# Thirteen phases in fp32r products: zero products at the start, tiles in steps of 256, fewer split products, and retention outputs in pairs

## The reference

```python
h = h + 0.5 * swiglu(rmsnorm(h, g), w_gate, w_up, w_down)        # FF = 2816

def hybrid_mixer(u, ...):
    q, k, v, a, b, g_sb, g_conv = split(u @ w_in)                 # 36 panels of 128 columns
    y_sb = stick_breaking_attention(q, k, v) @ w_attn_out
    y_conv = conformer_conv(a, b, ...) @ w_conv_out
    m = sigmoid(g_sb) * y_sb + sigmoid(g_conv) * y_conv
    return m @ w_out

def _retention(xn, w_in, subln, w_out):
    q, k, v, g = split(xn @ w_in)                                 # 4 heads, chunks of 128
    o = _rms(retain(q, k, v), subln)                              # 2048 wide
    return (silu(g) * o) @ w_out
```

## Time and profile before

| | us |
|---|---|
| median of 3 executions | 2171.73 (2171.69 to 2171.99) |
| the profiled execution | 2172.23 |
| its span | 2170.4 |
| TensorE busy | 2159.0 (18139 products) |
| VectorE busy | 1473.0 |
| ScalarE busy | 1202.2 |
| GpSimd busy | 283.9 |

### The profile page before, as it was taken

One profiled execution on the slowest core, in us unless ns is written; L12 is line 12 of the kernel. 1 busy time (PEld: TensorE's weight loads), 2 busy tenths in 40 slices (PEclk: granted clock), 3 DMA queues, 4 the chain that ended last, 5 costly groups with the idle time before them and its releaser, 6 DMA issues.

```text
span 2170.4 us, 48317 instructions
## 1 busy us (share of the span) xinstructions
PE 2159.0 (99%) x18139; PEld 2141.7 (99%) x18139; DVE 1473.0 (68%) x2242; ACT 1202.2 (55%) x1752; POOL 283.9 (13%) x328
## 2 busy tenths in 40 slices
PE   8999999999999999999999999999999999999999
PEld 8999999999999999999999999999999999999999
DVE  6655998665566579876657657976656745686663
ACT  6444786544444368755555546865445535565552
POOL 0001661100100136220020011010010010101000
PEclk9999999999999999999999999999999999999999
DMA  6555435556455554455656655356656655445664
GB/s 233 176 192 167 163 118 175 175 174 198 153 181 186 182 165 142 149 177 193 205 180 194 200 188 170 117 184 191 207 173 195 209 178 180 161 158 195 193 217 131
DMA packets 100401, 386.57 MB, mean 178 GB/s; under 512 B 11312, under 2 KB 12464, under 8 KB 100304
## 3 DMA queue, kind: packets, MB, share of 16 engines
q1 hardware_dynamic: 99648, 383.89, 53.7%
q0 software_dynamic: 368, 1.26, 0.2%
q10 hardware_dynamic: 288, 0.12, 0.0%
HBM read 384.18 MB, written 1.05 MB: 177 GB/s over the span
## 4 chain that ended last, share of the span: by engine, by line
PE 91%; DVE 6%; ACT 2%; issue 1%; DMA 0%; SPq 0%; ACTq 0%; DVEq 0%
PE bank L423 28%; PE bank L416 28%; PE bank L424 28%; DVE wlo L439 2%; DVE bank L1702 1%; PE bank L1056 1%; PE bank L1058 1%; PE bank L1057 1%; ACT whi L432 1%; PE bank L1103 0%; PE bank L770 0%; DVE proj L1688 0%; PE bank L947 0%; PE bank L950 0%; PE bank L949 0%
## 5 line engine op out<-in xcount | busy, mean ns | idle before, releaser
L416 PE MATMUL bank<-u,whi 128*128 128x256 f32 (+2 forms) x3776 | 1062.6, 281 | 7.3 <-DVE u L477 7.3
L423 PE MATMUL bank<-u,whi 128*128 128x256 f32 (+1 forms) x3776 | 1062.1, 281 | 0.0
L424 PE MATMUL bank<-u,wlo 128*128 128x256 f32 (+1 forms) x3776 | 1060.0, 281 | 0.0
L439 DVE TENSOR_TENSOR wlo<-raw,whi 128x1024 fp32r<-128x1024 f32 (+1 forms) x677 | 892.7, 1321 | 186.1 <-ACT whi L432 185.5
L432 ACT ACTIVATE whi<-raw 128x1024 fp32r<-128x1024 f32 (+1 forms) x677 | 743.5, 1112 | 192.3 <-PE bank L424 172.0
L416 PEld LDWEIGHTS bank<-u,whi 128*128 128x128 f32 x3776 | 711.3, 188 | 8.5 <-DVE wlo L439 7.2
L423 PEld LDWEIGHTS bank<-u,whi 128*128 128x128 f32 x3776 | 711.3, 188 | 0.9 <-issue 0.2
L424 PEld LDWEIGHTS bank<-u,wlo 128*128 128x128 f32 x3776 | 711.1, 188 | 0.0
L416 PE MATMUL bank<-hid,whi 128*128 128x256 f32 (+1 forms) x1408 | 394.2, 280 | 0.0
L423 PE MATMUL bank<-hid,whi 128*128 128x256 f32 (+1 forms) x1408 | 394.2, 280 | 0.0
L424 PE MATMUL bank<-hid,wlo 128*128 128x256 f32 (+1 forms) x1408 | 394.2, 280 | 0.0
(11 more groups left out here) (297 smaller groups left out, 2190.8 us busy)
## 6 DMA issues: line engine op xcount, KB each, us to landing
raw<-w SPq DMA_DIRECT2D x552, 512.0 KB, 3.3
raw<-w SPq DMA_DIRECT2D x128, 704.0 KB, 4.8
h<-xT SPq DMA_DIRECT2D x4, 272.0 KB, 5.6
outT<-h SPq DMA_DIRECT2D x8, 128.0 KB, 5.0
consts<-cst POOLq DMA_DIRECT2D x1, 576.0 KB, 5.0
dist<-cst POOLq DMA_DIRECT2D x1, 192.0 KB, 2.8
rdist<-cst POOLq DMA_DIRECT2D x1, 192.0 KB, 3.7
sgain<-small POOLq DMA_DIRECT2D x1, 145.5 KB, 5.4
```

The costliest lines, as they stand in the source:

```text
L416: pe.matmul(out[:, cut:cols], w, x[:, cut:cols], start=first, stop=False, skip_group_check=True)
L423: pe.matmul(out, w_h, x_lo, start=False, stop=False, skip_group_check=True)
L424: return pe.matmul(out, w_l, x_hi, start=False, stop=last, skip_group_check=True)
L439: dve.tensor_tensor(weights(1, n), raw[:, n % RING, 0:COLS[n]].rearrange("p (k c) -> p k c", c=128), weights(0, n), ALU.subtract).then_inc ...
```

## The change

It has five parts. (1) A memset of `sq` and five f32 products of zeros run on TensorE before anything is loaded; the order of the first loads is x, half of panel 0, x, the other half, x, x, then panels 1 to 3 in halves, and ScalarE, VectorE and TensorE work on the first four panels by halves. The first sum of squares goes from GpSimd to VectorE, and GpSimd's loads of constants wait for the fourth high part. (2) In the second mixer the inputs of the last products lie 256 columns apart (`mixed_at`, `attended_at`), and its weights 128. (3) `CUTS` is (0, 128, 0, 0): one product in two parts for each feed-forward, behind the norm. (4) `BEHIND_TERMS` has 7 entries, cut at 128; the mixer's input panels have one cut instead of two, and its end three new ones; attention's output tile 4 has one. (5) Retention's output tiles are made in pairs: the first eight terms for both, then the other eight for both, with a new order on ScalarE and VectorE.

```diff
-CUTS = (0, 252, 128, 0)
-BEHIND_TERMS = [(0, 1), (0, 2), *((t, c) for t in range(1, RT_HEADS + 1) for c in (0, 1)), (RT_HEADS, 5), (RT_HEADS + 1, 1), (RT_HEADS + 1, 2)]
+CUTS = (0, 128, 0, 0)
+BEHIND_TERMS = [(0, 1), *((t, 1) for t in range(1, RT_HEADS + 1)), (RT_HEADS, 5), (RT_HEADS + 1, 1)]
...
+        def mixed_at(l, part, k):
+            if l == 0:
+                return qk[:, KD * part + k, :]
+            at = KD * T * part + SEQ * k
+            return qk[:, :, :].rearrange("p a t -> p (a t)")[:, at:at + SEQ]
...
-            step = GAP_STEP if in_mixer_end(n) else 128
+            step = GAP_STEP if in_first_mixer_end(n) else 128
...
+            for i in range(X_PARTS):
+                sp.dma_start(h[:, X_TILES * i:X_TILES * (i + 1), :], ...).then_inc(x_loaded[i], 16)
+                if i < 2:
+                    load_half(0, i)
+            for n in range(1, RING):
+                for i in range(2):
+                    load_half(n, i)
...
+            pe.wait_ge(zeros_set, 1)
+            for i in range(WARM_UP):
+                pe.matmul(NORM[:, 0:SEQ], sq[:, 0:128], sq[:, 0:SEQ], start=True, stop=True)
...
             for f in range(KD):
                 act_update(act, 0, f)
-            act_split(act, 1)
-            act_split(act, 2)
+                if f in (1, 3):
+                    act_half(act, 0, f // 2)
+            for n in range(1, RING - 1):
+                for i in range(2):
+                    act_half(act, n, i)
...
-                out_proj(y, P + 48, 2)
+                for f in range(KD):
+                    n = P + 48 + 2 * f + RING
+                    act_split(act, n)
+                    act_split(act, n + 1)
+                    act_update(act, y + 1, f)
...
-                out_proj(y, P + 48, 2, 1.0, SEQ)
+                for f in range(KD):
+                    n = P + 48 + 2 * f + RING
+                    dve_split(dve, n)
+                    if f % 2 == 0:
+                        dve_split(dve, n + 1)
+                    if f > 0:
+                        dve_update(dve, y + 1, f - 1)
+                    dve.wait_ge(panel_used, P + 48 + 4 * (f // 2) + 3 + f % 2)
+                    dve.tensor_tensor(h[:, f, W], bank[4 + f % 2][:, 0:SEQ], h[:, f, W], ALU.add).then_inc(h_done, 1)
+                    if f % 2 == 1:
+                        dve_split(dve, n + 1)
+                dve_update(dve, y + 1, KD - 1)
```

More of the change, by code:

```diff
@@ L17 @@
 K8 = KD * 128
+HALF8 = K8 // 2
 K11 = HALF * 128
@@ L598, in _, with group @@
                   .then_inc(x_loaded[i], 16)
+                if i < 2:
[3 more added lines that the diff above has]
+                    load_half(n, i)
             def panels(n0, count, src, d0, cols):
[L603 to L604 removed]
+                def group(it):
+                    for j in range(RING):
                         n = n0 + j
[L606 to L607 removed]
+                        sp.wait_ge(lo_ready, n - RING + 1 + RING * it)
                         sp.dma_start(raw[:, n % RING, 0:cols], src[d0 + j + RING * it, :, :])\
                           .then_inc(raw_loaded[n % RING], 16)
[L610 to L613, removed]
+                with sp.Fori(1 if n0 == 0 else 0, count // RING) as it:
                     group(it)
@@ L643, in gate_up @@
                         n, g = b["P"] + j, b["A"] + j
-                        pe.wait_ge(lo_ready, n + 1 + RING * it)
+                        halves = norm and slow
+                        if halves:
+                            pe.wait_ge(half_lo, j + 1)
+                        else:
+                            pe.wait_ge(lo_ready, n + 1 + RING * it)
                         if g + RING * it >= RING if isinstance(it, int) else True:
@@ L647, in gate_up @@
                         for k in range(KD):
+                            if halves and k == KD // 2:
+                                pe.wait_ge(lo_ready, n + 1)
                             if norm and j == 0 and slow:
@@ L1113, in rt @@
                                       stop=True).then_inc(r_osum, 1)
-                out_proj(y, b["P"] + 48, 2, KD, lambda part, k: ry[:, part, k, :], r_y_ready,
-                         16, SEQ, lag=6)
+                with pe.Fori(0, KD // 2) as it:
+                    for q in range(2):
+                        for j in range(2):
+                            n = b["P"] + 48 + 2 * q + j
+                            if q == 0:
+                                pe.wait_ge(h_done, KD * (y + 1) + j - 1 + 2 * it)
+                            pe.wait_ge(lo_ready, n + 1 + RING * it)
+                            for k in range(KD):
+                                K = q * KD + k
+                                if j == 0 and (K == 0 or K >= KD):
+                                    pe.wait_ge(r_y_ready, KD if K == 0 else K + 1)
+                                mm = products(pe, bank[4 + j][:, 0:SEQ], n, k, ry[:, 0, K, :], ry[:, 1, K, :],
+                                              K == 0, K == 2 * KD - 1)
+                            mm.then_inc(panel_used, 1)
+            pe.wait_ge(zeros_set, 1)
+            for i in range(WARM_UP):
+                pe.matmul(NORM[:, 0:SEQ], sq[:, 0:128], sq[:, 0:SEQ], start=True, stop=True)
             layer = 0
```

89 lines of the change are left out of this document (57 added, 32 removed).

## The result

The changed kernel took 2182.17 us in the median of 18 executions (2169.49 to 2187.64); the kernel before, beside it, 2171.99 us (2170.94 to 2173.37, 18 executions). The ratio is 1.004, 95% interval 1.0031 to 1.0049: slower, where 2167.8 us was forecast. The spread says more than the median. The 18 times of before lie within 2.4 us. Those of the changed kernel lie in groups: 2169.49 once, five from 2175.96 to 2178.63, seven from 2181.97 to 2182.38, four from 2183.86 to 2184.69, and 2187.64. From the first group to the second and from there to the third it is 6 to 7 us; the four near 2184 and the one at 2187.64 fit such steps less well. The profiled execution took 2176.67 us (span 2174.9), so it is one of the second group; no execution of the groups above it was profiled.

The account below looks back on a forecast made before the run. TensorE bounds the kernel: instruction count times rhythm (113.3 or 118 ns) plus a few stalls. Terms -0.9 - 0.9 - 1.2 - 1.7 + 0.75 = -3.95 us, from the median 2171.73, gave 2167.8 us; range 2165.6 to 2170.4.

Parts of the forecast that it names:

- The step that failed: Feed-forwards: a 128 part right behind the norm brings back the 113.3 ns rhythm behind three norms, -0.3 us.
- rival (d): Feed-forwards: the 128 part behind a norm leaves the slow rhythm on, 7.0 us each, three giving 2188.8; chance 0.05.
- Second mixer's end: Steps of 256 bring the products behind the stall to 113.3 ns; less new parts and stalls, -1.2 us.
- Rival (a): Second mixer's end: the rhythm doesn't follow the tiles' steps, so the mixer gives 0: 2169.0; chance 0.13.
- Start: Kernel's start: zero products bring full clock near 6.5, the new load order the first norm at 16.95: -1.7 us.
- Retention's input: Retention's input panels: six parts fewer and faster rhythm, less some panels turning slow, -0.9 us (bounds -1.2 and -0.4).
- Outputs in twos: Retention's outputs: old stall gone, -0.35, but a new stall before the next norm, +1.1: net +0.75 us.
- Feed-forwards, the part I kept: Five feed-forwards of 256 columns: one part fewer in each, 0.113 us a part, -0.6 us together.
- Attention: Attention's outputs: a new part at f = 4, but VectorE sets the stage's end: 0, at most +0.11 us.

Follow-up runs that it names:

- e2: The changed kernel with a second 128+128 part, in panel 2 of each 256-column feed-forward, beside the one behind the norm: 2170.15 us.
- e4: The changed kernel with no product of a feed-forward in two parts: 2189.82 us.
- e5: e1 without the five zero products at the start: 2175.95 us.
- e8: e1 with the second mixer's end in its old tile steps, the changed kernel's parts kept: 2176.33 us.
- e16: e9 without the zero products at the start: 2169.62 us.
- e14: e9 with the second mixer's end in its old tile steps, parts kept: 2169.97 us.
- e11: e9 with the start of the kernel before (no zero products, whole loads and splits): 2170.20 us.
- e1: The changed kernel with each feed-forward's 128+128 part moved from panel 1, behind the norm, to panel 2, a running stream: 2169.65 us.
- e9: e7 with VectorE's eight products of h by the norm's factor in the second feed-forward spread over eight tiles instead of four: 2168.74 us.
- e6: e1 with six zero products at the start instead of five: 2170.35 us.
- e13: e9 with each feed-forward's 128+128 part back in panel 1, straight behind the norm's product: 2173.53 us.
- e7: e1 with VectorE's last u at the retention's end ahead of the low part instead of behind it: 2169.52 us.

## Why the prediction was wrong

**The step that failed** is in the feed-forwards: "With the 128 part right behind the norm, 22 products x 4.5 ns x 3 = -0.3 us", and the weight of rival (d), 0.05. The mechanism and price of (d) stood there: 1560 products x 4.5 ns = 7.0 us; the profile has 1557 slow products and +6.8. What I set against it, "every 128 part in the trace is followed by 113.3 within four products", was evidence from parts in a running stream alone, which the same paragraph says. Over all 18 profiles (kernels before and changed, and the experiments), leaving out mixers with the old steps, 158 parts of 128+128 stood behind at least six regular products. In panels of feed-forwards, mixer and retention 142 of 142 were followed by 113.3, and 83 of these streams had been slow. In attention's output tile 4 the part never lifted anything: 11 streams came fast and stayed so, 5 came slow (e2, e4, e5, e8, e16) and stayed slow. e2 there, TensorE:

```profile
1416.43 0.28 PE L922 MATMUL bank<-dy_hi,wlo 128*128 128x256 f32 x1
1416.56 0.22 PE L433 MATMUL bank<-dy_hi,dw_hi 128*128 128x128 f32 x1
1416.62 0.27 PE L435 MATMUL bank<-dy_hi,dw_hi 128*128 128x128 f32 x1
...
1417.72 0.28 PE L435 MATMUL bank<-dy_hi,dw_hi 128*128 128x256 f32 x1
1418.07 0.28 PE L435 MATMUL bank<-dy_hi,dw_hi 128*128 128x256 f32 x1
```

The last two starts lie 0.35 us apart over three products, 0.117 each. For comparison with the parts in a stream, here is the first product straight behind an f32 product of `ssq` (seven norms and two such sums a panel later in each profile), by its form:

| first product behind the norm | then fast | then slow |
|---|---|---|
| 128+128 | 33 | 2 |
| 252+4 | 5 | 6 |
| whole | 35 | 81 |

The places differ too, so the five feed-forwards by themselves: 128+128 was followed by fast products in 18 of 20 cases, whole in 32 of 65. At the first and the fourth, whole was slow in 24 of 26 and 128+128 fast in 8 of 8; at the other three the two did alike (30 of 39 and 10 of 12 fast). So the form of that product shifts the odds, and in a feed-forward only the running stream made it certain (no part there failed). The kernel before drew badly at three of its norms and ran only some 22 products slow each time, because a part in the running stream came one panel later; the change saved that part's 0.113 us and put 7.0 at stake five times. (The 23 in 2.40 us of the earlier trace rows, counted as the others, would give 114 ns; it is the starts there, 0.118 us apart, that show the slow rhythm.) At 7 in 50 that is 4.9 us per execution for 0.56 saved.

**What no rival had:** the wait inside the second feed-forward. The forecast priced a part fewer and a fast panel as TensorE's gain and never asked who comes second there. The chain of VectorE and ScalarE does. In the kernel before, TensorE came there 0.2 us later and just didn't wait; and what the wait costs is not its 0.1 us but, in three of seven profiles, the rhythm of all that follows.

**Second mixer's end,** -1.2 forecast, -1.10 by the traces, 1.23 by e14. The stall at 910.49 is there. Behind it the way to the norm takes 40.34 us against 41.29, 0.95 less and not 1.75. Most of the other 0.8 went to three things: the two parts and waits for VectorE, which were in the sum, and a slow stretch, which was not. TensorE waited 0.15 us at 924.83 and 0.08 at 927.94, and 35 products behind the second wait ran at 117.8 until the next part:

```profile
924.83 0.28 PE L442 MATMUL bank<-ao_hi,wlo 128*128 128x256 f32 x1
925.10 0.39 PE L434 MATMUL bank<-ao_hi,whi 128*128 128x256 f32 x1
...
927.94 0.36 PE L434 MATMUL bank<-qk,whi 128*128 128x256 f32 x1
928.13 0.28 PE L441 MATMUL bank<-qk,whi 128*128 128x256 f32 x1
```

Rival (a) falls: the steps count (e8, e14; 0.93 and 1.11 us by the traces).

**Start,** -1.7 forecast, -1.31 in this profile, 1.46 by e11. I put the clock near 6.5. In the changed kernel's profile the 272-column products lie 0.227 us apart until 10.7 and 0.12 after (1.2 and 2.4 GHz):

```profile
6.60:10.40 3.80, 3.80 (x17) 1.00 1.02 347
10.80:17.00 6.20, 6.20 (x52) 1.00 0.90 322
```

That is the exception: of the 13 profiles with zero products 11 have the 0.12 us spacing by 7.3, and only this one and e1's (10.3) have it late. But that the clock is there doesn't bring the norm forward by itself. In e9, with the same start, the full clock was there at 6.65, the first norm at 16.96 (forecast 16.95), and TensorE waited for data instead:

```profile
8.83 0.36 PE L435 MATMUL bank<-u,whi 128*128 128x272 f32 x1 [0.66 <-DVE u L511]
```

Against e9, the late clock cost 0.2 to 0.4 us (norm at 17.17 in e1, 17.38 in the changed kernel), late data 0.7 to 0.9 (e6 and e13: clock by 6.5, norm at 17.62 and 17.90). The forecast had reckoned with one arrival of the data; what it missed in most executions is how late they can be. Over the profiles with zero products the first norm lies between 16.96 and 17.90, and this scatter may be what blurs comparisons of under half a microsecond. The Trainium skill ("TensorE: Matmul & The Clock Gate", Part 1: The HAM clock gate) says that how many products run at the low clock differs between executions of one kernel; the traces agree (full clock at 6.65 in e9 and at 10.7 in the changed kernel, whose starts are the same code).

**Retention's input,** -0.9 forecast, -0.32 by both pairs of traces. The six parts (0.68) and the 70 products behind (4, 5) (0.31) were gained. I allowed +0.2 for panels that turn slow; three panels (t, 0) turned for 29 products each (0.39), panels (0, 2) and (0, 3) for 47 instead of 22 (0.11), (5, 0) for 23 (0.10): +0.60. These terms add up to -0.39. The stated bounds were -1.2 and -0.4, so the -0.32 lies just outside them.

**Outputs in twos,** +0.75 forecast, +0.90 measured: -0.35 to the hundredth, and the new stall with its place (three products before the norm), its releaser (VectorE's u) and its cause (e7). The changed kernel, VectorE and then GpSimd:

```profile
1984.75 0.42 DVE L2168 TENSOR_TENSOR h<-bank,h 128x256 f32<-128x256 f32 x1
1985.13 1.23 DVE L457 TENSOR_TENSOR wlo<-raw,whi 128x1024 fp32r<-128x1024 f32 x1
1986.27 0.83 DVE L510 SCALAR_TENSOR_TENSOR u<-h,gain,u 128x256 fp32r<-128x256 f32 x1
```

```profile
1985.24 1.58 POOL L545 TENSOR_TENSOR sq<-h 128x256 f32<-128x256 f32 x1 [2.04 <-DVE h L2168]
1986.90 0.79 POOL L548 TENSOR_TENSOR ssq<-ssq,sq 128x256 f32<-128x256 f32 x1
```

The order is the forecast one; what was lengthened is not the low part (1.23) but u (0.83, elsewhere 0.48), and GpSimd's square took 1.58, where the one at 1981.76, alone, took 0.62. It starts 0.11 behind the low part and ends 0.46 after it, about as if it had waited for the low part's end and only then run, though 0.46 is less than the 0.62 alone. The Trainium skill ("SBUF — State Buffer", Who interferes with whom) says that VectorE with two SBUF inputs contends with a GpSimd instruction that reads SBUF, and that the ports they share are an exclusive lock. I had set that below the row of 1.63; this pair of rows agrees with it roughly. The sum of squares, whose lateness I had not carried on to the norm, then held the norm by 0.1.

**Feed-forwards, the part I kept,** -0.1 to -0.2 each: four made -0.56. The part's 0.113 us is right. The Trainium skill ("TensorE: Matmul & The Clock Gate", Back-to-back issue gap) gives the formula that the prediction set beside it for an isolated product, and says that it under-counts small products in a stream; the traces agree, with 0.113 us for a part instead of 2.5 ns. **Attention,** 0 forecast, +0.02; its new part lifts nothing (above), and in the profiles where its outputs ran slow the stage took 118.42 to 118.52 us instead of some 118.2.

**In all,** with -0.2 for the last feed-forward at the fast rhythm the terms give -2.6 where -3.95 was forecast: 2169.2, beside the 2169.49 of the one execution without a slow stretch. Even without the failed step the forecast was 1.4 us too low, mostly from retention's input and the start. That 2169.2 would have been inside the stated range is no merit of these terms, of which two were off by 0.4 and 0.6.

## What to carry to other kernels

When a trace shows two rhythms, ask what sets the state at each place where the stream restarts, and keep the instruction that restores the good one in a running stream behind the last wait; straight behind the norm's product it only shifts the odds. Read from the trace, place by place, that it does restore it: here it did in the panels and not in attention's outputs. Before saving time on the bounding engine, find who comes second in each stage and by how much: a wait of 0.1 us could cost 5.9 here. Take the spread of many executions as seriously as their median, since one profile can land in any of the groups, and read a term of a few tenths from its own stretch of the trace, not from the total.

## What the hardware showed that was not expected

- A rhythm that is drawn when the stream restarts and then holds for 160 us: 113.3 or 117.8 ns for products of 256 columns, at a clock column of 1.00, over 1557 products (changed kernel) and 1318 (e5, e7). Behind the same wait of 0.1 us it was slow in three profiles and fast in four.
- The draw follows small differences. By their times e4 was slow in three feed-forwards in each of its five executions, e13 in none to two.
- A 128+128 part in a running stream turned 83 of 83 slow streams fast where panel weights met `u` or `qk` tiles, and none of 5 in attention's outputs.
- The tile steps make a rhythm of their own, 117.6 ns on average, that the parts don't lift (e8, e14).
- GpSimd's square of 128 x 256 took 1.58 us beside VectorE's low part and 0.62 alone.
- What inside TensorE holds the slow rhythm stays open; no run here looks into it.
